# Value and gate units of an input projection taken in overlapping pairs

## The reference, cut to what matters

```python
z = h @ w_in
u, v, q, k, val, g_f, g_b = jnp.split(z, IN_SPLITS, axis=-1)
a_out = _chunk_gmlp(jax.nn.gelu(u), jax.nn.gelu(v), w_s, b_s, vnorm_gain)
...
y_f, y_b, s_new = _retention_bidir(qh, kh, heads(val, B_DV), decay_param, s0)
b_out = jax.nn.silu(g_f) * merge(y_f) + jax.nn.silu(g_b) * merge(y_b)
return jnp.concatenate([a_out, b_out], axis=-1) @ w_out, s_new
```

## Time and profile before

| | |
|---|---|
| time, median of 3 runs | 2465.24 us (2464.73 to 2471.47) |
| span of the profiled execution | 2463.1 us |
| median of the runs less that span | 2.1 us |
| instructions | 38831 |
| PE busy | 2414.4 us (98%) |
| ACT, DVE, POOL busy | 794.3, 1577.4, 989.5 us |
| units 8 to 13 | 292.35 to 493.04 us |

### The profile page before, as it was taken

The page is one execution under the profiler, slowest core; times in us unless marked ns, Lnnn a source line. Parts: engine busy times, 40 slices in busy tenths (PEclk is TensorE's granted clock), DMA queues, the critical chain, the costliest instruction groups (busy, mean ns, idle before and its releaser), DMA issues.

```text
span 2463.1 us, 38831 instructions
## 1 busy us (share of the span) xinstructions
PE 2414.4 (98%) x13994; PEld 2120.1 (86%) x13994; DVE 1577.4 (64%) x2578; ACT 794.3 (32%) x1250; POOL 989.5 (40%) x520
## 2 busy tenths in 40 slices
PE   7999999989999999999999999999999999999998
PEld 5988999988888888888888888888888888888887
DVE  6666732284487878877787886578333337877764
ACT  4322131151233223223222322764333334333322
POOL 0135321173023333333333333027665667775740
PEclk9999999999999999999999999899999999999999
DMA  8334433384212211121211121033343446343322
GB/s 293 120 129 154 137 99 107 121 277 167 78 41 84 72 60 60 61 101 60 77 60 60 60 97 40 18 116 108 123 132 123 132 170 223 129 145 123 123 86 86
DMA packets 152260, 274.12 MB, mean 111 GB/s; under 512 B 7364, under 2 KB 98280, under 8 KB 151272
## 3 DMA queue, kind: packets, MB, share of 16 engines
q1 hardware_dynamic: 149200, 263.22, 31.4%
q10 hardware_dynamic: 2968, 9.63, 1.2%
HBM read 204.66 MB, written 63.96 MB: 109 GB/s over the span
## 4 chain that ended last, share of the span: by engine, by line
PE 89%; DVE 6%; ACT 2%; issue 1%; DMA 1%; POOL 0%; SPq 0%; DVEq 0%; ACTq 0%; POOLq 0%
PE bank L517 84%; PE bank L2642 1%; PE bank L2545 1%; DMA hL_f<-in_ada_w_dram 1%; DVE X L1846 1%; PE bank L2898 1%; PE bank L2438 1%; PE bank L2732 0%; DVE G1L L2322 0%; DVE ada_acc_mlp L1838 0%; DVE xgm L2045 0%; DMA gt<-gate_spill 0%; ACT yn L1110 0%; PE bank L2596 0%; DVE h1L L2052 0%
## 5 line engine op out<-in xcount | busy, mean ns | idle before, releaser
L1846 DVE SCALAR_TENSOR_TENSOR X<-bank,mod,X 128x512 f32<-128x512 f32 (+1 forms) x852 | 544.8, 684 | 237.6 <-PE bank L517 237.5
L1490 POOL TENSOR_TENSOR ringL<-stage,ringH 128x2048 fp32r<-128x2048 f32 x64 | 306.6, 4790 | 634.2 <-ACT ringH L911 634.2
L517 PE MATMUL bank<-hH,ringH 128*128 128x512 f32 (+1 forms) x1248 | 447.6, 359 | 0.2 <-DVE hL L2052 0.2
L517 PE MATMUL bank<-hH,ringL 128*128 128x512 f32 (+1 forms) x1248 | 442.4, 354 | 0.0
L517 PE MATMUL bank<-hL,ringH 128*128 128x512 f32 (+1 forms) x1248 | 441.9, 354 | 0.0
L517 PEld LDWEIGHTS bank<-hH,ringL 128*128 128x128 f32 x1248 | 235.9, 189 | 33.2
L517 PEld LDWEIGHTS bank<-hH,ringH 128*128 128x128 f32 x1248 | 236.0, 189 | 33.0 <-DVE hL L2052 1.0
L517 PEld LDWEIGHTS bank<-hL,ringH 128*128 128x128 f32 x1248 | 236.2, 189 | 32.2
L911 ACT ACTIVATE ringH<-stage 128x2048 fp32r<-128x2048 f32 x65 | 124.1, 1909 | 301.8 <-PE bank L517 291.4
L517 PE MATMUL bank<-ringH,hH 128*128 128x256 f32 x640 | 184.8, 289 | 0.4 <-DVE hL L1817 0.3
L517 PE MATMUL bank<-ringH,hL 128*128 128x256 f32 x640 | 181.1, 283 | 0.0
(11 more groups left out here) (407 smaller groups left out, 5720.3 us busy)
## 6 DMA issues: line engine op xcount, KB each, us to landing
stage<-in_mlp_w_dram SPq DMA_DIRECT2D x64, 1024.0 KB, 5.6
ada_st_mlp<-in_ada_w_dram SPq DMA_DIRECT2D x18, 1536.0 KB, 8.2
stage<-in_ev_w_in_dram SPq DMA_DIRECT2D x14, 1024.0 KB, 5.9
mid_spill<-midT SPq DMA_DIRECT2D x56, 256.0 KB, 2.2
ada_st_in<-in_ada_w_dram SPq DMA_DIRECT2D x8, 1536.0 KB, 10.3
mid_spill<-midB SPq DMA_DIRECT2D x48, 256.0 KB, 2.0
gate_spill<-gate_st ACTq DMA_DIRECT2D x8, 640.0 KB, 3.5
gt<-gate_spill SPq DMA_DIRECT2D x20, 256.0 KB, 3.4
```

The lines of the kernel that those rows point to most:

```text
L517: mm = nc.tensor.matmul(out, a, b, start=first and n == 0, stop=last and n == 2, skip_group_check=chained)
L1490: nc.gpsimd.tensor_tensor(ringL[slot][:, :], stage[:, :], ringH[slot][:, :].bitcast(F32), ALU.subtract).then_inc(w_lo, 1)
L1846: V.scalar_tensor_tensor(out=X[:, d, cols(t)], in0=src[:, 0:TB[t][1]], scalar=gate_ap, in1=X[:, d, cols(t)], op0=ALU.mult, op1=ALU.add).th ...
```

## The change

The units 8 and 9, 10 and 11, 12 and 13 are taken in overlapping pairs. The first unit of a pair does 3 (val) or 4 (gates) token tiles alone, 256 columns wide. For the remaining 7 or 6 tiles one moving operand takes the columns of both slots of the ring, 512 wide. The second unit then does alone the 3 or 4 tiles that the first had begun with. Units 8 to 13 have 41 groups in place of 60: 22 of 256 columns and 19 of 512. PE waits for the second unit's low half ahead of the first pair.

The gates leave by a ring of four tiles of [128, 2, 256] with a store behind each of the 28 gate groups, and two semaphores in turn. In units 10 and 12 ACT splits the next unit's weights behind the second group, not the first. The state steps follow the gate groups by number (keys behind group 8, values behind 9, and so on to 25), the last ada total stands behind gate group 7, and POOL's clearing of the states now comes ahead of the split of the first output unit.

```diff
+FIRST_GATE = 10
+ALONE = {8: 3, 10: 4, 12: 4}
+IN_GROUPS = [ALONE.get(u - 1, NT) if tok else NTB * HT for u, (_, _, _, tok) in enumerate(IN_UNITS)]
+GATE_STEPS = (IN_CUM[N_IN] - IN_CUM[FIRST_GATE]) // 2
+def two_units(ui, g):
+    return ui in ALONE and g >= ALONE[ui]
-R_UNITS = {11: range(0, 4), 12: range(4, 7), 13: range(7, 10)}
+R_STORES = {10: range(0, 2), 11: range(2, 5), 12: range(5, 10)}
+R_FIRST = 8
+LAST_ADA_AT = 7
...
+    ring = at("ring", A_R0, [P, 2, 2, 2048], F32R)
+    ringH, ringL = ([ring[:, i, part, :] for i in range(2)] for part in range(2))
-    gate_st = at("gate_st", A_M, [P, NT, UC])
+    gate_st = [at(f"gate_st{i}", A_M + 2 * i, [P, 2, UC]) for i in range(4)]
...
# ACT
+                        step = G - IN_CUM[FIRST_GATE]
...
+                        if step % 2 == 0:
+                            after(act, gate_out[step // 2 % 2], 32 * (step // 4))
+                        dst = gate_st[step % 4][:, half:half + 1 + both, :]
+                        ev = nc.scalar.activation(dst.rearrange("p h n -> p (h n)"), src, ACT.Silu)
...
-                if kind in ("gf", "gb") and g % (NT // 2) == NT // 2 - 1:
+                if kind in ("gf", "gb"):
                     act.wait_ge(in_ev, G)
...
+                    q0 = (ui - FIRST_GATE) // 2 * 2 + half
+                    act.dma_start(g_dram[q0:q0 + 1 + both, :, g, :].rearrange("h p n -> p h n"), dst).then_inc(gate_out[step // 2 % 2], 16)
-                if g == 0 and ui > 0:
+                if g == (1 if ui in ALONE and ui >= FIRST_GATE else 0) and ui > 0:
                     split_static(ui + 1)
...
# PE
+                if two_units(ui, g) and g == ALONE[ui]:
+                    pe.wait_ge(w_lo, ui + 2)
                 for k in range(DT):
-                    if tok:
+                    if two_units(ui, g):
+                        ts = slice(g * P, (g + 1) * P)
+                        mm = pair_pass(bank[G % 4].rearrange("p (s n) -> p s n", s=2), ring[:, :, 0, k * UC:(k + 1) * UC], ring[:, :, 1, k * UC:(k + 1) * UC],
+                                       hH[:, k, ts], hL[:, k, ts], k == 0, k == DT - 1, weights_moving=True)
+                    elif tok:
...
+                step = G - 1 - IN_CUM[FIRST_GATE]
+                if step == LAST_ADA_AT:
+                    ada_in_total(ADA_IN_UNITS[9])
+                n, half_of = divmod(step - R_FIRST, 2)
+                if 0 <= n < len(ADVANCE):
+                    (state_keys, state_values)[half_of](ADVANCE[n])
```

More of the change, by code:

```diff
@@ L53 @@
 U_POOL = U_MLP[1] - 1
-IN_GROUPS = [NT if tok else NTB * HT for _, _, _, tok in IN_UNITS]
+ALONE = {8: 3, 10: 4, 12: 4}
+IN_GROUPS = [ALONE.get(u - 1, NT) if tok else NTB * HT for u, (_, _, _, tok) in enumerate(IN_UNITS)]
 IN_CUM = [sum(IN_GROUPS[:i]) for i in range(N_IN + 1)]
+GATE_STEPS = (IN_CUM[N_IN] - IN_CUM[FIRST_GATE]) // 2
+def two_units(ui, g):
+    return ui in ALONE and g >= ALONE[ui]
 VEC_AT = 4
@@ L261, in build @@
     midL = at("midL", A_M + 10, [P, HT, T], F32R)
-    ringH = [at(f"ringH{i}", a, [P, 2048], F32R) for i, a in enumerate((A_R0, A_R1))]
-    ringL = [at(f"ringL{i}", a + 8, [P, 2048], F32R) for i, a in enumerate((A_R0, A_R1))]
+    ring = at("ring", A_R0, [P, 2, 2, 2048], F32R)
+    ringH, ringL = ([ring[:, i, part, :] for i in range(2)] for part in range(2))
     stage = at("stage", A_ST, [P, 2048])
@@ L451, in build @@
     rope_in, swap_in, rot_s, rot_c, rot_ok, gate_out = (sem("rope_in"), sem("swap_in", 2), sem("rot_s"), sem("rot_c"),
-                                                        sem("rot_ok"), sem("gate_out"))
+                                                        sem("rot_ok"), sem("gate_out", 2))
     pos_in, tab_exp, tab_ok, state_in, zero_ok = sem("pos_in"), sem("tab_exp"), sem("tab_ok"), sem("state_in"), sem("zero_ok")
@@ L702, in _ @@
                     sp.dma_start(S[d][0][:, :, :], state_ret[0, 0, d].rearrange("h d e -> d h e")).then_inc(state_in, 16)
-            for st in R_UNITS.get(v, ()):
+            for st in R_STORES.get(v, ()):
                 for d in range(2):
@@ L748, in _ @@
         state_loads(1)
-        sp.wait_ge(gate_out, 32 * 4)
+        for s in gate_out:
+            sp.wait_ge(s, 16 * GATE_STEPS)
         gate_loads(0)
@@ L1019, in swap_halves @@
                 act.dma_start(swap[hd % 2][a:a + P // 2, :], qk[b:b + P // 2, hd, 0:SAMPLE]).then_inc(swap_in[hd % 2], 16)
-        G, gates = 0, 0
+        G = 0
         for ui, (kind, half, _, tok) in enumerate(IN_UNITS):
@@ L1042, in _ @@
                 if tok:
-                    src = first_bank(g) if ui == 0 else bank[G % 4][:, 0:UC]
-                    lo, hi = half * UC, (half + 1) * UC
+                    both = two_units(ui, g)
+                    src = first_bank(g) if ui == 0 else bank[G % 4][:, 0:UC * (1 + both)]
+                    lo, hi = half * UC, (half + 1 + both) * UC
                     if kind == "v":
@@ L1052, in _ @@
                     else:
-                        if g == 0:
+                        step = G - IN_CUM[FIRST_GATE]
+                        if step == 0:
                             act.wait_ge(rot_ok, 2 * HEADS)
-                            after(act, gate_out, 32 * gates)
-                        ev = nc.scalar.activation(gate_st[:, g, :], src, ACT.Silu)
+                        if step % 2 == 0:
+                            after(act, gate_out[step // 2 % 2], 32 * (step // 4))
+                        dst = gate_st[step % 4][:, half:half + 1 + both, :]
+                        ev = nc.scalar.activation(dst.rearrange("p h n -> p (h n)"), src, ACT.Silu)
                 else:
@@ L1089, in _ @@
                 swap_halves(1)
-            if kind in ("gf", "gb"):
-                gates += 1
         for k in range(NT + 3):
@@ L1504, in _ @@
         for ui, (kind, half, _, tok) in enumerate(IN_UNITS):
+            if ui == 13:
+                for d in range(2):
+                    pool.wait_ge(s_ok, 2 * advances_before(NS - 1))
+                    pool.wait_ge(s_out[0], 16 * NS)
+                    nc.gpsimd.memset(S[d][NS % 2][:, :, :], 0.0).then_inc(zero_ok, 1)
             if ui > 0:
@@ L1525, in _ @@
                                             base=0, pattern=[[0, HEADS], [sign, P]], channel_multiplier=-sign).then_inc(tab_ok, 1)
[L1526 to L1531, removed]
         pool.wait_ge(tab_ok, 2)
@@ L1994, in _ @@
             if k == 2:
-                dve.wait_ge(gate_out, 32 * 4)
+                for s in gate_out:
+                    dve.wait_ge(s, 16 * GATE_STEPS)
             if k < NT:
@@ L2600, in _ @@
                         ada_in_total(ADA_IN_UNITS[ui - 1])
[L2601 to L2605, removed]
+                step = G - 1 - IN_CUM[FIRST_GATE]
[4 more added lines that the diff above has]
+                    (state_keys, state_values)[half_of](ADVANCE[n])
+            if ui - 1 in ADA_IN_UNITS and ui < FIRST_GATE and not (kind == "u" and half == 1):
                 ada_in_total(ADA_IN_UNITS[ui - 1])
```

2 lines of the change are left out of this document (removed).

## The result

The changed kernel takes 2475.66 us (median of 4 runs, 2475.36 to 2476.78); the kernel before took 2465.83 (2464.73 to 2471.47) beside it. The ratio is 1.0038 with a 95% interval of 1.0027 to 1.005: slower by some 9.8 us. The span of the profiled execution went from 2463.1 to 2473.6 us, +10.5. The forecast was 2480.0 us in a range of 2470 to 2487, with 0.85 on slower.

A forecast was written before the change was run, and what follows sets the result against it. PE was taken as the bound, never stopping in units 8 to 13. Pairs -6.0, waits +2.2, +3.2 and +11.9, clock +2.5 and +1.0 gave +14.8 us of span: 2480.0 us, range 2470 to 2487.

The forecast's parts named there:

- Rival C: Units 8 to 13: second units' low halves are done before the first pairs, no waits, 2459.2 us; chance 0.06.
- The pairs: Units 8 to 13: nineteen products groups of 512 columns save 0.315 us each on PE, -6.0 us.
- rival B: Pairs in units 8 to 13: waits as forecast, and the two-run operand costs up to 6.0 us, 2486; chance 0.08.
- First wait: Unit 8's first pair: PE waits 2.2 us for POOL's low half of unit 9.
- Second wait: Unit 10's start: PE waits 3.2 us for its low half, which POOL finishes behind DVE's batch.
- Third wait: Unit 10's first pair: PE waits 11.9 us for unit 11's low half, late through Exp, ada load and DVE batch.
- Rival A: Unit 10: POOL isn't held up by DVE's batch, wait 7.0 to 9 us, sum +9.5, 2474.7 us; chance 0.17.
- The clock: PE's granted clock falls after the gaps: 2.5 us after the 11.9 us one, 1.0 after the 2.2 us one.
- No loss from the stores and totals: Gate stores, last total and stage end in units 8 to 13: hidden, between -0.6 and +0.6 us, taken as 0.
- rival D: Retention stage behind: gives gap costs back through earlier SP loads, at most 5 us, +6, 2471, no change; chance 0.09.

The follow-up runs named there:

- e5: Changed kernel with four groups of unit 8 alone instead of three and the next unit's split behind the first group again: 2459.51 us, ratio 0.9973.
- e2b: Changed kernel with no unit run as a pair and the state stores redistributed over units 11 and 12: 2464.33 us, ratio 0.9991.
- e7: Changed kernel with DVE's batch in unit 9 held until unit 10's low half is written, its total moved into unit 10: 2470.54 us, ratio 1.0013.
- e6: Changed kernel with only one number changed, four groups of unit 8 unpaired instead of three: 2471.68 us, ratio 1.0018.
- e1: Changed kernel with the next unit's split behind the first group again, ahead of the Exp, in units 10 and 12: 2465.81 us, ratio 0.9997.
- e2: Changed kernel with no pairs, the state stores left in the changed kernel's places on SP: 2472.12 us, ratio 1.0024.
- e4: Changed kernel with 30 unused products of 512 columns put ahead of PE's wait in unit 10: 2473.23 us, ratio 1.0027.
- e3: Changed kernel with eight groups of unit 10 alone instead of four, so four pairs fewer: 2466.22 us, ratio 1.0.

## Why the prediction was right, and what was off

The mechanism was right at each place: three waits, in order, with the third the largest, none in unit 12 (unit 13's low half was written at 446.28 and the pair began at 449.00, 2.7 us of cover for 2.8 forecast), and low clock behind the large one. Rival C falls with the waits. The stage ended 10.9 us later where some 14 were forecast, and the step from +14.8 to +10.5 is in the sizes.

- **The pairs, -6.0: they were -5.1.** The second run of columns costs nothing that the trace shows (5.48 us a pair in the piece of 38.35 us, 5.465 forecast), so rival B falls. But a pair gives 0.27 us and not 0.315 (e5 against e2b). The forecast took a group of 256 columns as 28.90 / 10 = 2.89 us, which has in it what a unit loses once at its start; a group between two others takes 2.87 to 2.88 us in the same chain, and some pairs take 5.49 to 5.61.
- **First wait, 2.2: it was 1.6.** Unit 8 started 0.6 us earlier than before, and POOL's rotation, which the forecast held fixed, ended at 294.4 instead of 298.3: the low half started at 296.99, behind ACT, where it was 298.27 behind POOL's own work. PE's three groups ended 0.6 earlier too.
- **Second wait, 3.2: it was 2.9.** The low half of 7.73 us beside the batch came as forecast from rows 5 and 6. That it was held to the batch's end was likely, not certain: the forecast says that POOL ended 4.5 us behind the batch in both splits it met, but the first line of rows 5, 4.93 us at 298.27, is a third one, and there POOL got in between the sums, as in unit 8 here (under e7).
- **Third wait, 11.9: it was 8.4.** This is the mis-sized term. Its mechanism held: Exp first, then the batch, then POOL 4.35 us behind it (4.5 forecast). Two things shortened it. The ada load was issued at 355.04, where I had 356.3, and DVE began 8.9 us later, not 10.0, so the pair started at 377.0 instead of 379.3. And PE reached the wait at 368.6 instead of 367.4, since it did its first group at a low clock.
- **Rival A** (POOL not held by the batch; 2474.7, though its own terms with 7.0 us of wait add to +9.9, which is 2475.1) is nearest in time and wrong in mechanism: the 5.84 us pass, e6's 9.43 and e7's 4.59 show the hold. So the time alone would have spoken for the wrong account.
- **The clock, 3.5: it was 3.7**, split otherwise. I had charged the first gap 1.0 and the third 2.5; the first (1.6 us) cost nothing, the third 1.4. The second cost 2.3, which I had left out of the sum because the third wait's end does not hang on PE. That end did not move, but the 2.3 belong to the sum as soon as the wait is counted from PE's own arrival, 368.6. Counted from PE's arrival at full clock, some 366.3, the third wait is 10.7 us with this clock loss in it, and 11.9 is to be read against that. Waits and clock together: 16.5 us for 20.8 forecast. With the pairs' -5.1, the earlier start of unit 8 (-0.6), the part behind the stage (-0.4) and the 0.2 not assigned, that is the +10.5 within the rounding.
- **No loss from the stores and totals.** Right (e2b). SP's wait for the last gate store in the stage behind fell from 5.0 us to 0.3, and the part behind the stage took 0.4 us less, within the ±0.6 and within what it differs by from profile to profile; nothing like the 5 us of rival D was given back.

What stays open: when POOL gets in between DVE's sums and when it is held to their end; the 0.2 us that no term holds; and why the part behind the stage is 1.8 us longer in e1 than in before. The 0.6 us by which unit 8 starts earlier do not come from the pairs: e2b, which has none, starts it at 291.71 too, and the first long piece of products is already 0.7 us earlier (80.43 us before, 79.77 in the changed kernel).

## What to carry to other kernels

Two units merged into one wide operand are worth what the wide product saves, but they ask for the second unit's inputs six or seven groups earlier than before; before merging, work out when each of those inputs arrives from what its own load and its own engines wait for, and move the producer's step ahead of anything long on its engine in the same edit (here one index: +9.8 us without it, -6.6 us with it and one pair fewer). A pass of POOL on the critical path is to be timed against the SBUF sums of DVE beside it, since it can end 4.35 us behind their last one and not 4.6 us behind its own start. An ablation that moves an order must take its queue places along: e2's 7 us came from stores left in the place that fitted another order.

## What the runs showed of the hardware

- POOL's 128x2048 subtraction and DVE's 128x384 sums of two tensors, all from SBUF, block each other. In units 9 and 10 POOL was held to the end of the whole chain of sums, not for one instruction: a pass begun 5.1, 3.4 or 1.5 us before the end of the batch ended 4.35 us behind it (9.43, 7.72 and 5.84 us instead of 4.6). In unit 8 a pass begun in the middle of a batch took 4.87 us, and one sum took 4.93 us instead of 0.61. In the batches of units 9 and 10 that held POOL, no sum had been held before; in unit 8's, in all ten profiles, POOL's rotation had already held one of the batch's sums (1.90 us in the changed kernel). Whether that decides it was not tested.
- The granted clock fell to 0.50 with waits of 2.4 (kernel before), 2.9, 5.8 (e7), 8.4 and 12.0 us (e6), and stayed at 1.00 with those of 1.2 (e7) to 1.7 us (e4). With the wait of 2.9 us it fell before the wait's end in the changed kernel and in e4, and in e1 and e3 only about when PE was at work again (0.70 and 0.74 in the slice of 354 to 356 us, then 0.50); the same gap cost 2.3 us in the changed kernel and some 1.2 in e1. Products put into the long wait (e4) kept the clock whole behind it.
- A moving operand of two runs of 256 columns 16 KB apart is as fast as one run of 512: 5.48 us and 5.465 us for 24 products. 24 products of 256 columns take 2.87 to 2.88 us.
